# MLP up projection with the weights as the stationary operand and 256 tokens moving

## What is computed

```python
def rms_norm(x, g, eps=NORM_EPS):
    xf = x.astype(jnp.float32)
    y = xf * lax.rsqrt(jnp.mean(xf * xf, axis=-1, keepdims=True) + eps)
    return (y * g.astype(jnp.float32)).astype(x.dtype)

def sq_relu_mlp(u, w_up, w_down):          # w_up 2048 x 8192, w_down 8192 x 2048
    return jnp.square(jax.nn.relu(u @ w_up)) @ w_down
...
        u = rms_norm(h, mlp_pre_g[i])
        h = h + rms_norm(sq_relu_mlp(u, w_mlp_up[i], w_mlp_down[i]), mlp_post_g[i])
```

## Time and profile before

| what | us |
| --- | --- |
| median of 3 executions | 2634.14 |
| lowest and highest | 2631.92, 2640.20 |
| the profiled execution | 2640.08 |
| its span, first to last instruction | 2638.3 |
| TensorE busy | 2525.6 (96%) |
| VectorE busy | 1423.3 (54%) |
| ScalarE busy | 1081.1 (41%) |

### The profile page before, as it was taken

One profiled execution on the slowest core, in us unless ns is written; L12 is line 12 of the kernel. 1 busy time (PEld: TensorE's weight loads), 2 busy tenths in 40 slices (PEclk: granted clock), 3 DMA queues, 4 the chain that ended last, 5 costly groups with the idle time before them and its releaser, 6 DMA issues.

```text
span 2638.3 us, 33540 instructions
## 1 busy us (share of the span) xinstructions
PE 2525.6 (96%) x14359; PEld 2091.0 (79%) x14359; DVE 1423.3 (54%) x1481; ACT 1081.1 (41%) x1169; POOL 172.8 (7%) x181
## 2 busy tenths in 40 slices
PE   8999989989999999999998998898999999999997
PEld 6888768778888878878877977787888888888875
DVE  5556774655544545445555667645544545545554
ACT  5445420454434334334444443545433434334442
POOL 3001243000000000000100000010000000000100
PEclk9999999989999999999999999998999999999999
DMA  7556402346565555555643655155555555555643
GB/s 246 191 175 215 155 26 99 113 159 227 181 195 185 189 174 179 192 174 185 197 160 110 204 168 167 58 195 197 177 193 191 189 191 191 185 195 177 193 161 109
DMA packets 224818, 453.22 MB, mean 172 GB/s; under 512 B 7833, under 2 KB 16343, under 8 KB 223403
## 3 DMA queue, kind: packets, MB, share of 16 engines
q1 hardware_dynamic: 218816, 430.11, 50.3%
q0 software_dynamic: 3648, 17.54, 2.0%
q10 hardware_dynamic: 2219, 3.59, 0.5%
HBM read 445.52 MB, written 2.10 MB: 170 GB/s over the span
## 4 chain that ended last, share of the span: by engine, by line
PE 93%; DVE 4%; ACT 2%; issue 1%; DMA 0%; ACTq 0%; SPq 0%; DVEq 0%
PE psum L294 28%; PE psum L296 27%; PE psum L295 27%; PE psum L602 1%; PE psum L717 1%; PE psum L318 1%; PE psum L1510 1%; PE psum L1491 1%; PE psum L1506 1%; ACT junk L386 1%; PE psum L848 0%; PE psum L849 0%; PE psum L850 0%; DVE h L451 0%; PE psum L1482 0%
## 5 line engine op out<-in xcount | busy, mean ns | idle before, releaser
L276 DVE TENSOR_TENSOR wlo<-raw,whi 128x2048 fp32r<-128x2048 f32 (+1 forms) x406 | 932.8, 2304 | 781.8 <-ACT whi L271 781.5
L271 ACT ACTIVATE whi<-raw 128x2048 fp32r<-128x2048 f32 (+1 forms) x408 | 773.9, 1902 | 803.7 <-DMA raw<-in_w_mlp_down 336.3
L294 PE MATMUL psum<-whi,uTh 128*128 128x512 f32 (+2 forms) x2176 | 856.2, 393 | 13.7 <-DVE uTl L342 7.3
L295 PE MATMUL psum<-wlo,uTh 128*128 128x512 f32 (+2 forms) x2176 | 845.3, 388 | 5.9 <-issue 5.9
L296 PE MATMUL psum<-whi,uTl 128*128 128x512 f32 (+2 forms) x2176 | 845.1, 388 | 0.0
L294 PEld LDWEIGHTS psum<-whi,uTh 128*128 128x128 f32 x2176 | 411.6, 189 | 102.1 <-issue 11.6
L295 PEld LDWEIGHTS psum<-wlo,uTh 128*128 128x128 f32 x2176 | 411.8, 189 | 87.5 <-issue 8.8
L296 PEld LDWEIGHTS psum<-whi,uTl 128*128 128x128 f32 x2176 | 411.2, 189 | 82.3
L294 PE MATMUL psum<-whi,hTh 128*128 128x512 f32 x1024 | 399.9, 390 | 0.0
L296 PE MATMUL psum<-whi,hTl 128*128 128x512 f32 x1024 | 398.6, 389 | 0.0
L295 PE MATMUL psum<-wlo,hTh 128*128 128x512 f32 x1024 | 398.4, 389 | 0.0
(11 more groups left out here) (354 smaller groups left out, 1453.2 us busy)
## 6 DMA issues: line engine op xcount, KB each, us to landing
raw<-in_w_mlp_up SPq DMA_DIRECT2D x128, 1024.0 KB, 5.2
raw<-in_w_mlp_down SPq DMA_DIRECT2D x128, 1024.0 KB, 5.1
raw<-in_ab_w_in SPq DMA_DIRECT2D x48, 1024.0 KB, 5.3
raw<-in_w_ple_gate SPq DMA_DIRECT2D x32, 1024.0 KB, 5.1
raw<-in_c_w_in SPq DMA_DIRECT2D x24, 1024.0 KB, 5.2
raw<-in_ab_w_out SPq DMA_DIRECT2D x16, 1024.0 KB, 5.1
raw<-in_c_w_out SPq DMA_DIRECT2D x16, 1024.0 KB, 5.0
raw<-in_c_w_in SPq DMA_DIRECT2D x12, 736.0 KB, 4.4
```

What stands on the lines that cost most here:

```text
L271: act.activation(whi[:, q, :, 0:n], raw[:, q, :, 0:n], ACT.Copy).then_inc(hi_ready, 1)
L276: dve.tensor_tensor(wlo[:, q, :, 0:n], raw[:, q, :, 0:n], whi[:, q, :, 0:n].bitcast(F32), ALU.subtract).then_inc(lo_ready, 1)
L294: pe.matmul(o, xh, hi, start=(q == 0 and k == 0), stop=False)
L295: pe.matmul(o, xh, lo, start=False, stop=False)
```

## The change

`mm_up` takes the place of `mm_slab` in the up slabs. The stationary operand is now a 128x128 piece of the weights, and all 256 tokens of `uTh` or `uTl` move. The same slab has 4 chunks by 4 row groups by 4 weight pieces `f` by 3 matmuls, 192 matmuls of 256 columns. The sums come out as hidden columns by tokens, in the form in which the down projection reads them, so `T_mlp_pe` and its transposes are gone. ReLU is applied without the factor, VectorE squares in two halves, and ScalarE and VectorE split `hid` directly, right behind the ReLU and the square of the same slab. Tokens now lie along the free dimension, where a factor per partition can't be applied. `rstd_h` becomes the squared factor (a reciprocal in place of the reciprocal root), and VectorE applies it where it takes up the down sums.

```diff
--- before.py
+++ after.py
@@ -143,7 +143,7 @@
 
     m = at("m", [P, TT, D], F32, 120)
     gpost = at("gpost", [P, D], F32, 136)
-    hid = at("hid", [P, 2, TT, W], F32, 144)
+    hid = at("hid", [P, 2, 4, T], F32, 144)
     hTh = at("hTh", [P, KT, T], F32R, 152)
     hTl = at("hTl", [P, KT, T], F32R, 168)
     wple = at("wple", [P, 2, D], F32, 184)
@@ -243,8 +243,8 @@
               "h_sq": lambda st: 8 if st in GAIN else 0, "rstd": lambda st: 1 if st in GAIN else 0}
     for kind in ("xT", "xT_hi", "xT_lo"):
         counts[kind] = lambda st: 8
-    for kind in ("sq_done", "hT", "hT_hi", "hT_lo", "ev_up", "ev_dn"):
-        counts[kind] = lambda st: 16 if st.startswith("mlp") else 0
+    for kind, n_ in (("ev_up", 32), ("sq_done", 32), ("hT_hi", 32), ("hT_lo", 16), ("ev_dn", 16)):
+        counts[kind] = lambda st, n_=n_: n_ if st.startswith("mlp") else 0
     for kind, n_ in (("gated", 4), ("emb", 4), ("ev_ple", 4), ("ple_in", 32), ("pT_mm", 1), ("pT", 1)):
         counts[kind] = lambda st, n_=n_: n_ if st.startswith("ple") else 0
 
@@ -486,7 +486,12 @@
                 split_lo(dve, s, b, n)
         if gain is not None:
             dve.wait_ge(*mark("h_sq", st, 8))
-            rstd_from(dve, link, hss[:], rstd_h[:], D, NORM_EPS).then_inc(sem("rstd"), 1)
+            if st.startswith("mlp"):
+                link(dve.tensor_reduce(rstd_h[:], hss[:], AX.X, ALU.add))
+                link(dve.tensor_scalar(rstd_h[:], rstd_h[:], 1.0 / D, NORM_EPS, ALU.mult, ALU.add))
+                dve.reciprocal(rstd_h[:], rstd_h[:]).then_inc(sem("rstd"), 1)
+            else:
+                rstd_from(dve, link, hss[:], rstd_h[:], D, NORM_EPS).then_inc(sem("rstd"), 1)
 
     def prologue(fn, eng, st):
 
@@ -590,55 +595,78 @@
         return width(nxt[st]) if nxt[st] and not st.endswith("_in") else None
 
 
-    def T_mlp_pe(pe, l, Q, j):
-
-        pe.wait_ge(*mark("sq_done", f"mlp{l}", 4 * Q + j + 1))
-        if j >= 2:
-
-            pe.wait_ge(*mark("hT_lo", f"mlp{l}", 4 * Q + j - 1))
-        for pr in range(2):
-            for kk in range(2):
-                for tt in range(TT):
-                    last = pe.transpose(bank[4 + 2 * (j % 2) + pr][:, (2 * kk + tt) * P:(2 * kk + tt + 1) * P],
-                                        hid[:, j % 2, tt, (2 * pr + kk) * P:(2 * pr + kk + 1) * P], ident[:])
-        last.then_inc(sem("hT"), 1)
-
-    def T_mlp_split(eng, l, Q, j, high):
-
-        eng.wait_ge(*mark("hT" if high else "hT_hi", f"mlp{l}", 4 * Q + j + 1))
-        for pr in range(2):
-            k = 4 * j + 2 * pr
-            x = bank[4 + 2 * (j % 2) + pr][:]
-            if high:
-                last = eng.activation(hTh[:, k:k + 2, :], x, ACT.Copy)
-            else:
-                last = eng.tensor_tensor(hTl[:, k:k + 2, :], x, hTh[:, k:k + 2, :].bitcast(F32), ALU.subtract)
-        last.then_inc(sem("hT_hi" if high else "hT_lo"), 1)
+    def mm_up(pe, s, par_, free, before=None):
+
+        pe.wait_ge(*free)
+        for q in range(4):
+            if before:
+                before(q)
+            pe.wait_ge(lo_ready, 4 * s + q + 1)
+            for k in range(4):
+                for f in range(4):
+                    o = bank[2 * par_ + f // 2][:, (f % 2) * T:(f % 2 + 1) * T]
+                    hi, lo = whi[:, q, k, f * P:(f + 1) * P], wlo[:, q, k, f * P:(f + 1) * P]
+                    xh, xl = uTh[:, 4 * q + k, :], uTl[:, 4 * q + k, :]
+                    pe.matmul(o, hi, xh, start=(q == 0 and k == 0 and f % 2 == 0), stop=False)
+                    pe.matmul(o, hi, xl, start=False, stop=False)
+                    last = pe.matmul(o, lo, xh, start=False, stop=(q == 3 and k == 3 and f % 2 == 1))
+            last.then_inc(mm_used, 1)
+
+    def relu_act(act, l, Q, j, par_):
+
+        for hf in range(2):
+            act.activation(hid[:, j % 2, 2 * hf:2 * hf + 2, :], bank[2 * par_ + hf][:],
+                           ACT.Relu).then_inc(sem("ev_up"), 1)
+
+    def square_dve(dve, l, Q, j):
+
+        for hf in range(2):
+            dve.wait_ge(*mark("ev_up", f"mlp{l}", 8 * Q + 2 * j + hf + 1))
+            x = hid[:, j % 2, 2 * hf:2 * hf + 2, :]
+            dve.tensor_tensor(x, x, x, ALU.mult).then_inc(sem("sq_done"), 1)
+
+    def hT_hi_act(act, l, Q, j):
+
+        for hf in range(2):
+            k = 4 * j + 2 * hf
+            act.wait_ge(*mark("sq_done", f"mlp{l}", 8 * Q + 2 * j + hf + 1))
+            act.activation(hTh[:, k:k + 2, :], hid[:, j % 2, 2 * hf:2 * hf + 2, :],
+                           ACT.Copy).then_inc(sem("hT_hi"), 1)
+
+    def hT_lo_dve(dve, l, Q, j):
+
+        for hf in range(2):
+            k = 4 * j + 2 * hf
+            dve.wait_ge(*mark("hT_hi", f"mlp{l}", 8 * Q + 2 * j + hf + 1))
+            last = dve.tensor_tensor(hTl[:, k:k + 2, :], hid[:, j % 2, 2 * hf:2 * hf + 2, :],
+                                     hTh[:, k:k + 2, :].bitcast(F32), ALU.subtract)
+        last.then_inc(sem("hT_lo"), 1)
 
     def mlp_pe(pe, l, Q):
         st = f"mlp{l}"
         s = base[st] + 8 * Q
         par_ = lambda r: (base[st] + r) % 2
-        up = lambda v: mark("ev_up", st, v)
+        up = lambda v: mark("ev_up", st, 2 * v)
         dn = lambda v: mark("ev_dn", st, v)
         first = isinstance(Q, int)
         if first:
-            pe_first(pe, st, s, par_(0), h_src, h_ready(st), W, free_of(st, 0))
-            mm_slab(pe, s + 1, par_(1), W, free_of(st, 1))
+            T_pe(pe, st, h_src, h_ready(st), 0)
+
+            def before(q):
+                if q < 3:
+                    T_pe(pe, st, h_src, h_ready(st), q + 1)
+                pe.wait_ge(*mark("xT_lo", st, 2 * q + 2))
+            mm_up(pe, s, par_(0), free_of(st, 0), before)
+            mm_up(pe, s + 1, par_(1), free_of(st, 1))
         else:
-            mm_slab(pe, s, par_(0), W, dn(4 * Q - 1))
-            mm_slab(pe, s + 1, par_(1), W, dn(4 * Q))
+            mm_up(pe, s, par_(0), dn(4 * Q - 1))
+            mm_up(pe, s + 1, par_(1), dn(4 * Q))
         for j in (2, 3):
-            T_mlp_pe(pe, l, Q, j - 2)
-            mm_slab(pe, s + j, par_(j), W, up(4 * Q + j - 1))
-        T_mlp_pe(pe, l, Q, 2)
-
-        def before(q):
-            if q == 2:
-                T_mlp_pe(pe, l, Q, 3)
-
+            mm_up(pe, s + j, par_(j), up(4 * Q + j - 1))
+
+        def down(q):
             pe.wait_ge(*mark("hT_lo", f"mlp{l}", 4 * Q + q + 1))
-        mm_slab(pe, s + 4, par_(4), W, up(4 * Q + 3), before, (hTh, hTl))
+        mm_slab(pe, s + 4, par_(4), W, up(4 * Q + 3), down, (hTh, hTl))
         mm_slab(pe, s + 5, par_(5), W, up(4 * Q + 4), None, (hTh, hTl))
         mm_slab(pe, s + 6, par_(6), W, dn(4 * Q + 1), None, (hTh, hTl))
         mm_slab(pe, s + 7, par_(7), W, dn(4 * Q + 2), None, (hTh, hTl))
@@ -650,16 +678,10 @@
         for r in range(8):
             s, j, par_ = base[st] + 8 * Q + r, r % 4, (base[st] + r) % 2
 
-            def relu():
+            def hidden():
                 act.wait_ge(mm_used, 4 * s + 4)
-                if first and r == 0:
-                    act.wait_ge(*mark("rstd", st, 1))
-                for tt in range(TT):
-                    last = act.activation(hid[:, j % 2, tt, :], bank[2 * par_ + tt][:], ACT.Relu,
-                                          scale=rstd_h[:, tt:tt + 1])
-                last.then_inc(sem("ev_up"), 1)
-                if j:
-                    T_mlp_split(act, l, Q, j - 1, True)
+                relu_act(act, l, Q, j, par_)
+                hT_hi_act(act, l, Q, j)
 
             def squares():
 
@@ -667,8 +689,7 @@
                 for tt in range(TT):
                     square(act, m[:, tt, j * W:(j + 1) * W], ssq[:, tt, j:j + 1], *mark("m_sq", st, 2 * j + tt + 1))
             step(split_hi, act, s, st, W,
-                 relu if r < 4 else squares if final else None, skip=first and r == 0,
-                 mid=(lambda: T_mlp_split(act, l, Q, 3, True)) if r == 4 else None)
+                 hidden if r < 4 else squares if final else None, skip=first and r == 0)
 
     def mlp_dve(dve, l, Q):
         st = f"mlp{l}"
@@ -677,21 +698,22 @@
         for r in range(8):
             s, j, par_ = base[st] + 8 * Q + r, r % 4, (base[st] + r) % 2
 
-            def square():
-                dve.wait_ge(*mark("ev_up", f"mlp{l}", 4 * Q + j + 1))
-                x = hid[:, j % 2, :, :]
-                dve.tensor_tensor(x, x, x, ALU.mult).then_inc(sem("sq_done"), 1)
-                if j:
-                    T_mlp_split(dve, l, Q, j - 1, False)
+            def hidden():
+                square_dve(dve, l, Q, j)
+                hT_lo_dve(dve, l, Q, j)
 
             def add():
                 dve.wait_ge(mm_used, 4 * s + 4)
+                if first and r == 4:
+                    dve.wait_ge(*mark("rstd", st, 1))
                 for tt in range(TT):
-                    x, y = bank[2 * par_ + tt][:], m[:, tt, j * W:(j + 1) * W]
-                    last = dve.tensor_copy(y, x) if first else dve.tensor_tensor(y, y, x, ALU.add)
```

(8 more changed lines are left out.)

## The result

| | median, us | ratio to the kernel before, 95% interval |
| --- | --- | --- |
| before, four executions | 2635.3 | |
| after, four executions | 2649.1 (2647.9 to 2650.7) | 1.0052 (1.0036 to 1.0067) |

The changed kernel is slower by 0.5%, 13.7 us (9 to 18). The forecast was 2653 in a range of 2630 to 2690. The profiled execution took 2647.9 us, 7.8 more than that of before; the single executions of each kernel spread over several microseconds, so the ratio tells the difference better than these two.

A forecast was written before the change was run, and what follows sets the result against it. TensorE's own stream was taken to bound the kernel. Terms 47.1 - 28.6 + 0 + 0.3 = +18.8 us put the profiled execution at 2658.9 us and the median at 2653, range 2630 to 2690.

The forecast's parts named there:

- up slabs: TensorE's 32 up slabs: 6144 matmuls of 256 columns at 121 ns in place of 3072 at 226.7 ns, +47.1 us.
- transposes: 32 groups of eight in TensorE's stream, 0.89 us each, all gained when removed: -28.6 us.
- loop starts: Starts of quarters 2 and 3: both layers fetch instructions again, four starts instead of two, 0 us against 15.7 before.
- factor on the down sums: VectorE's squared factor, hidden but for the last slab of each layer: +0.3 us in both layers.
- the surplus: Time of an fp32r matmul beyond its columns, 13.4 to 13.8 ns, claimed not to shrink with the width.
- the tie: Stationary load about as long as the stream at 256 columns; step taken as 121 ns, a little over 120.5.
- The floor: Load of a 128x128 stationary operand can be renewed every 112 ns at least, read from fp32 matmuls of L2169.
- Rival 2: Up slabs: renewing the fp32r load takes 126 to 140 ns, +78 to +164 us, 2684 to 2770 us; chance 0.15.
- Rival 1: Up slabs: surplus isn't the matmul's, 109 to 112 ns a step, 2579 to 2598 us; chance 0.12, 0.08 for 113 to 118 ns.
- the count of instructions: Packets of 256 instructions place the second stop at a loop start: 41 matmuls on in layer 0, 28 in layer 1.
- lower bound of -4: Low end of the loop-start term, in us, for four starts without any loss of clock.
- What lies beside: Work beside TensorE: ScalarE free some 2.9 us behind an up slab instead of 2.3, costing TensorE nothing.

The follow-up runs named there:

- b_256: Kernel before, tokens stationary and transposes kept, each up matmul cut into two of 256 weight columns: 2680.6 us, ratio 1.0164.
- b_shift: Kernel before with 30 transposes that nobody reads added in layer 0, ahead of the loop over quarters: 2629.2 us, ratio 0.9966.

## Why the prediction was right, step by step

The ledger, forecast against what was measured:

| term | forecast, us | measured, us | by |
| --- | --- | --- | --- |
| up slabs | +47.1 | +41.0 | 6144 x 0.1200 - 696.3 |
| transposes | -28.6 | -27.8 | 8 x 3.48, kept in the changed kernel, in a stretch without a jump |
| loop starts | 0 | -1.6 | 14.1 against 15.7 in the windows |
| factor on the down sums | +0.3 | -2.9 to +3.7 | 1.0001 (0.9989 to 1.0014) |
| all | +18.8 | +13.7 (9.5 to 17.7) | 1.0052 (1.0036 to 1.0067) |

The measured terms add up to some 12 us, which lies inside the interval of the whole. The two kernels with their quarters written out differ by the same 12.0 us without any loop start.

**The up slabs.** That the surplus belongs to the matmul and not to its columns was the step on which the sign hung, and it held: 213.3 + 13.4 ns, 153.3 + 13.8 and 106.7 + 13.3 at the three widths. b_256 shows that it doesn't depend on which operand moves. What was mis-sized was the tie: I gave 0.5 to 1 ns for a load that is as long as the stream, read from the fp32 rows of 256 and 128 columns. There is none. The floor is 112 ns, as read from L2169, and lies under 120. That 1 ns is 6 us, as much as the 5 us by which the sum was too high. Rival 2, the load as the bound, didn't come true at 256 columns; at 128 the step was that of the floor. Rival 1, no surplus, has nothing left for it.

**The transposes.** In TensorE's stream with nothing idle beside them, so their time came back in full. Kept, they cost 27.8 us by the stretch without a jump, where 28.6 was forecast (32 x 0.89 is 28.5). The 27.4 us by the two ratios hold other losses at loop starts too and prove less.

**The loop starts.** Four in place of two, with a short second stop: the count of instructions put it 41 matmuls on in layer 0 and 28 in layer 1, with 0.3 and 2.0 us. In quarter 3 of the trace it stood 40 and 27 matmuls on, with 0.33 and 1.56 us. In quarter 2 the clock fell first, so the matmuls ahead took longer and the packet was nearly or fully in time: no second stop in layer 0, 0.40 us in layer 1. Of the forecast's 15.6 us 14.1 came, and the parts missed in opposite directions: the first stops 8.1 for 8.0, the second ones 2.3 for 4.6, the clock and the rest 3.7 for 3. So the fit of this term is in part luck. Its lower bound of -4 was also a little too low by its own sum: without any loss of clock it is 12.6 - 15.7 = -3.1. The count was tried in turn by b_shift, which moved the stops from one layer to the other.

**What lies beside.** ScalarE was free 2.7 us behind a slab's end, where 2.9 was worked out, and TensorE waited for none of it.

## What to carry to other kernels

Where TensorE is the bound, compare two layouts by the number of matmuls first: at equal columns, each fp32r matmul added costs its fixed 13.3 ns, here 3072 x 13.3 = 41 us, and a layout that saves 256 transposes (some 28 us) doesn't earn that back. A loop in TensorE's program is worth writing out when its body lies over more packets of instructions than stay loaded: it brought 0.5% here for the kernel before, about as much as the change cost. And a stop that the profile names after an engine may be the program's own: look whether the same wait stands elsewhere without a stop, and at the instruction queue.

## What was not expected of the hardware

A stream of fp32r matmuls of 128 columns, at the floor of 112 ns a step, kept TensorE at full clock (1.00 over 171.5 us), but where a stop of some 2 us had brought the clock to half, as three of four did, the same stream left it there for 327 us, at 213 ns a step. It came back some 5 us behind the start of the next matmuls of 512 columns (0.97 over 89 us). With 256 columns the clock came back inside the up matmuls, 3.4 us behind both falls of the changed kernel, and 6.8 us behind the two of the kernel before with its matmuls cut in two.

The starts of a loop cost different amounts from one to the next at the same place in the code (3.7 and 2.5 us in layer 0 of the changed kernel, 8.7 and 7.0 before), since the clock fell at one and not, or for less long, at the other.
